# Forget gates of one attention layer: gate columns as the stationary operand on four column groups, tokens moving

## What is computed

```python
def fox_attention(h, w_in, f_bias, w_o):          # h: [1, 256, 1024], w_in: [1024, 3*1024 + 16]
    proj = h @ w_in
    q, k, v, f = jnp.split(proj, [D, 2 * D, 3 * D], axis=-1)      # f: [1, 256, 16], one gate a head
    log_f = jax.nn.log_sigmoid(f.astype(jnp.float32) + f_bias.astype(jnp.float32))
    F = jnp.cumsum(log_f, axis=1).transpose(0, 2, 1)
    ...
        logits = jnp.einsum('bhqd,bhkd->bhqk', qb, k).astype(jnp.float32) * scale
        logits = logits + Fq[..., :, None] - F[:, :, None, :]
    ...
```

## Time and profile before

| what | value |
|---|---|
| time, median of 3 runs | 2028.2 us (2025.67 to 2031.05) |
| profiled execution: span, first to last instruction | 2030.4 us |
| mean granted TensorE clock in it | 0.912 |
| instructions | 25040 |
| PE / PEld / DVE / ACT / POOL busy | 81% / 48% / 36% / 13% / 5% |
| HBM read | 578.88 MB, 286 GB/s over the span |

### The profile page before, as it was taken

How to read it: one execution, slowest core, us unless ns; L and a number is a source line. 1 busy time by engine, 2 the same in 40 slices (tenths; PEclk the granted TensorE clock), 3 DMA queues, 4 the chain that set the end, 5 groups by cost and what they waited for, 6 DMA issues and landing times.

```text
span 2030.4 us, 25040 instructions
## 1 busy us (share of the span) xinstructions
PE 1648.7 (81%) x10030; PEld 984.7 (48%) x10031; DVE 738.1 (36%) x1492; ACT 258.5 (13%) x630; POOL 94.1 (5%) x125
## 2 busy tenths in 40 slices
PE   5999987766665678876667547989999999999998
PEld 3754543222222254322222214766997486669963
DVE  2865452111101136211111003974467313444672
ACT  1002210000000021000000002232111122311100
POOL 1001001000000002910000000000000000000000
PEclk9989998888877799987887778999999999999999
DMA  9979479999999996999999987204435273204351
GB/s 362 402 314 413 172 305 412 421 422 422 422 422 422 405 389 272 415 405 422 421 422 422 422 332 291 84 1 176 166 125 207 104 259 144 105 11 166 125 209 40
DMA packets 122680, 581.33 MB, mean 286 GB/s; under 512 B 10820, under 2 KB 15272, under 8 KB 67160
## 3 DMA queue, kind: packets, MB, share of 16 engines
q1 hardware_dynamic: 120416, 573.92, 70.6%
q0 software_dynamic: 1104, 2.86, 0.4%
q10 hardware_dynamic: 1064, 3.17, 0.4%
HBM read 578.88 MB, written 1.05 MB: 286 GB/s over the span
## 4 chain that ended last, share of the span: by engine, by line
PE 35%; DMA 33%; PEld 14%; DVE 8%; issue 5%; ACT 2%; SPq 2%; PEldq 1%; DVEq 1%; ACTq 0%
DMA ring_buffer<-in_exp_w 29%; PEld ps L2175 10%; PE ps L1479 7%; PE ps L2204 6%; PE ps L1504 4%; PE ps L2893 4%; PE ps L2004 3%; DMA ring_buffer<-in_ada_w 2%; PEld ps L2146 2%; DMA ring_buffer<-in_attn_w_in 1%; PE ps L1004 1%; PE ps L2884 1%; SPq L1368 1%; PEld ps L831 1%; DVE xn L537 1%
## 5 line engine op out<-in xcount | busy, mean ns | idle before, releaser
L1479 PE MATMUL ps<-ring_buffer,arena 128*32 128x512 f32 x1984 | 295.8, 754 | 173.5 <-DMA ring_buffer<-in_exp_w 170.6
L1479 PEld LDWEIGHTS ps<-ring_buffer,arena 128*32 128x32 f32 x1984 | 76.8, 134 | 379.1 <-issue 324.7
L1504 PE MATMUL ps<-ring_buffer,arena 128*32 128x512 f32 x1088 | 151.8, 709 | 86.7 <-DMA ring_buffer<-in_exp_w 75.5
L1675 DVE TENSOR_TENSOR arena<-arena,ps 128x512 f32<-128x512 f32 x18 | 19.1, 1064 | 407.5 <-PE ps L1479 407.5
L2175 PE MATMUL ps<-arena,ring_buffer 128*128 128x128 f32 x1152 | 133.9, 276 | 3.7 <-issue 3.7
L2175 PEld LDWEIGHTS ps<-arena,ring_buffer 128*128 128x128 f32 x1152 | 130.8, 192 | 5.8 <-issue 5.8
L1504 PEld LDWEIGHTS ps<-ring_buffer,arena 128*32 128x32 f32 x1088 | 40.4, 127 | 186.8 <-issue 146.9
L2204 PE MATMUL ps<-ring_buffer,arena 128*128 128x512 f32 x252 | 111.0, 594 | 3.4 <-issue 1.9
L2175 PE MATMUL ps<-hT,ring_buffer 128*128 128x128 f32 x864 | 99.4, 275 | 0.0
L2175 PEld LDWEIGHTS ps<-hT,ring_buffer 128*128 128x128 f32 x864 | 97.9, 192 | 0.0
L1693 DVE TENSOR_TENSOR arena<-ps,gates 128x512 f32<-128x512 f32 x16 | 11.1, 692 | 193.7 <-PE ps L1504 193.7
(11 more groups left out here) (570 smaller groups left out, 2061.0 us busy)
## 6 DMA issues: line engine op xcount, KB each, us to landing
ring_buffer<-in_exp_w SPq DMA_DIRECT2D x376, 1024.0 KB, 18.6
ring_buffer<-in_ffn_w SPq DMA_DIRECT2D x30, 2048.0 KB, 11.8
ring_buffer<-in_ada_w SPq DMA_DIRECT2D x24, 2048.0 KB, 17.4
ring_buffer<-in_c_w_in SPq DMA_DIRECT2D x8, 2048.0 KB, 13.8
ring_buffer<-in_attn_w_in SPq DMA_DIRECT2D x6, 2048.0 KB, 16.0
arena<-in_exp_w SPq DMA_DIRECT2D x6, 1024.0 KB, 8.4
ring_buffer<-in_ab_w_in SPq DMA_DIRECT2D x3, 2048.0 KB, 14.1
ring_buffer<-in_ffn_w SPq DMA_DIRECT2D x6, 1024.0 KB, 6.3
```

What stands on the lines that cost most here:

```text
L1479: ins = pe.matmul(ps[c, bank, :], tokens[:, 4 * phase + k, c], halves[j][:, k, :], start=(phase == 0 and k == 0), stop=(phase == 1 and k = ...
L1504: ins = pe.matmul(ps[c, bank, :], tokens[:, 2 * phase + k, c], halves[j][:, k, half * 512:(half + 1) * 512], start=(phase == 0 and k == 0) ...
```

## The change

The gates are computed the other way round. The 16 gate columns of piece k are stationary and all 256 tokens move, and piece k goes to the column group 32 * (k % 4) of the array, so that the products of four pieces write to four different groups of PSUM partitions. Each group sums two pieces (k and k + 4). The four partial sums, with gates on partitions and tokens along the row, are copied by DVE to SBUF (`gate_parts`, in the buffer `probs`). Two products with `gate_parts` stationary (128 tokens each) and 16 columns of `fold` moving add the four groups and turn the result, so that tokens are on partitions as before. They go to bank 0, columns 64 to 95, and are placed in PE's order after the first two of the eight pieces of tile 17. DVE takes its bias addition from there. The counts of two semaphores move up by one. The wait for bank 0 moves from `gate_sums_pe` to the new `gate_fold_pe`.

```diff
+            gate_parts = probs[:, 0, 0, :]
+
+            def gate_fold_pe(pe):
                 bank_free(pe, SUM_BANK)
                 pe.wait_ge(gate_rows, 1)
+                for t in range(TT):
+                    ins = pe.matmul(ps[:, SUM_BANK, 64 + 16 * t:80 + 16 * t], gate_parts[:, t * P:(t + 1) * P],
+                                    const("fold")[:, 0:N_HEADS], start=True, stop=True)
+                ins.then_inc(gate_sums, 1)
+
+            def gate_sums_pe(pe):
+                pe.wait_ge(gate_rows, 2)
...
                 bank_free(pe, bank_of(F_TILE), F_TILE)
-                for t in range(TT):
-                    for k in range(KD):
-                        ins = pe.matmul(ps[:, bank_of(F_TILE), t * 16:(t + 1) * 16], hT[:, k, t * P:(t + 1) * P], w[:, k, :],
-                                        start=(k == 0), stop=(k == KD - 1))
+                for k in range(KD):
+                    g = 32 * (k % 4)
+                    ins = pe.matmul(ps[g:g + N_HEADS, bank_of(F_TILE), 0:S], w[:, k, :], hT[:, k, :],
+                                    start=(k < 4), stop=(k >= 4))
                 ins.then_inc(p_ready, 1)
                 release(pe)
                 w = ring.take(pe, ("attn_in", 4))
-                values_pe(pe, 17, w, 0, range(KD))
+                values_pe(pe, 17, w, 0, range(2))
+                gate_fold_pe(pe)
+                values_pe(pe, 17, w, 0, range(2, KD))
...
                 dve.wait_ge(p_ready, F_TILE + 1)
+                dve.tensor_copy(gate_parts, ps[:, bank_of(F_TILE), 0:S]).then_inc(gate_rows, 1)
                 dve.wait_ge(bias_loaded, 16)
-                v(dve.tensor_tensor(t1, ps[:, bank_of(F_TILE), 0:32].rearrange("p (t h) -> p t h", t=TT),
+                dve.wait_ge(gate_sums, 1)
+                v(dve.tensor_tensor(t1, ps[:, SUM_BANK, 64:96].rearrange("p (t h) -> p t h", t=TT),
                                     fbias.unsqueeze(1).to_broadcast([P, TT, N_HEADS]), ALU.add))
...
```

More of the change, by code:

```diff
@@ L798, in bank_free @@
                     pe.wait_ge(p_taken, before[-1] + 1)
-            def gate_sums_pe(pe):
+            gate_parts = probs[:, 0, 0, :]
+            def gate_fold_pe(pe):
                 bank_free(pe, SUM_BANK)
                 pe.wait_ge(gate_rows, 1)
+                for t in range(TT):
[4 more added lines that the diff above has]
+                pe.wait_ge(gate_rows, 2)
                 pe.matmul(ps[:, SUM_BANK, 0:16], const("upto"), lf[:, 0, :], start=True, stop=True)
@@ L807, in gate_turn_pe @@
             def gate_turn_pe(pe):
-                pe.wait_ge(gate_rows, 2)
+                pe.wait_ge(gate_rows, 3)
                 for t in range(TT):
@@ L907, in proj_dve @@
                 values(18)
-                dve.wait_ge(gate_sums, 1)
+                dve.wait_ge(gate_sums, 2)
                 dve.tensor_copy(F, ps[:, SUM_BANK, 0:32].rearrange("p (t h) -> p t h", t=TT)).then_inc(gate_rows, 1)
@@ L911, in proj_dve @@
                 condition_unit(9)
-                dve.wait_ge(gate_sums, 2)
+                dve.wait_ge(gate_sums, 3)
                 for row in (0, 32):
```

## The result

The changed kernel takes 2011.06 us (median of 8 runs, 2007.97 to 2014.6), the kernel before 2021.98 us (8 runs, 2013.17 to 2031.05). The ratio is 0.9948, with a 95% interval of 0.9925 to 0.9972. A second measurement, with more runs of both, gave 0.9951 (0.9929 to 0.9973). So the change makes the kernel faster by 0.5%, some 10 us, where 5.4 were forecast (2022.8 against 2028.2, a ratio of 0.9973). The median of the kernel before had itself come down from 2028.2 (three runs) to 2022.0 (eight) and later 2020.2 (35): the forecast of the saving and the base it was taken from were both off.

A forecast was written before the change was run, and what follows sets the result against it. No single limit: PE and transfers each hold a third of the wait chain, PE's pace sets the projection stage's end. 3.46 (products) - 0.5 (fold) + 2.45 (clock) = 5.4 us; 2028.2 - 5.4 = 2022.8 us, range 2018.6 to 2028.1.

The forecast's parts named there:

- Products: Gate products on PE: eight on four column groups take 1.32 us where the old took 4.78, saving 3.46 us.
- Fold and its cover: Two fold products on PE add 0.5 us; 0.9 us of cover from tile 17 hides the wait for DVE's copy.
- Rival 5: The fold waits for a late DVE copy, PE idles 4.3 us and the clock falls; 2029.6 us, chance 0.03.
- Clock: Tiles 17 and 18 behind the gates run at full clock, saving 2.45 us (bounds 0 and 2.45).
- The rival that the fall isn't in every execution: The clock falls anyway, or other executions didn't lose by it; gain 3.0 us, 2025.2 us, chance 0.24.
- the stated bounds of 4.5 to 5.6: Range put around the forecast saving of 5.4 us, which was given a chance of 0.50.
- What is late next: Behind the gates' stage: the full 5.4 us passes through conditioning transfers, heads and expert loads to the kernel's end.
- Rival 3: The saving is given back later by expert loads that start when they did; 2028.2 us, chance 0.08.
- rival 2: The column groups don't overlap: gates take 3.8 us, gain 2.9 us; 2025.3 us, chance 0.04.
- Rival 4: More than forecast: clock falls at 136.3 and the heads' start move to where they cost nothing; 2021.1 us, chance 0.11.
- The size: Whole kernel: 5.4 us less than the 2028.2 us median of three runs, so 2022.8 us.

The follow-up runs named there:

- fold_first: Changed kernel with the fold right behind the gate products, ahead of all of tile 17, so nothing covers DVE's copy; ratio 0.9962, median 2013.29 us.
- before: The kernel before, without the change; median 2021.98 us of 8 runs.
- before_plus2: Kernel before with two small products, result unused, added behind PE's first transposes to move its later code; ratio 0.9985.
- before_plus10: Kernel before with ten small products, result unused, added behind PE's first transposes to move its later code; ratio 0.9978.
- pad58: Kernel before with 58 small products, result unused, added behind PE's first transposes to move its later code; ratio 1.0032.
- bunch: Changed kernel with the sixteen old narrow gate products put back as dead work ahead of the new ones; 2023.73 us, one run.
- after_again: Changed kernel measured and traced once more, no edit; ratio 0.9951, median 2011.32 us of 12 runs.
- before_third: Kernel before traced a third time, no edit, one run; the execution of 2022.93 us.
- after: The changed kernel in its first measurement and trace; ratio 0.9948, median 2011.06 us of 8 runs.
- pad6: Changed kernel with six small products, result unused, behind PE's first transposes, giving PE as many products as the kernel before; ratio 0.9973.
- after_plus5: Changed kernel with five small products, result unused, added behind PE's first transposes; ratio 0.9968.
- before_again: Kernel before measured and traced a second time, no edit; ratio 1.0002, median 2019.71 us of 12 runs.
- one_group: Changed kernel with all eight gate products on the first column group and the fold taking that group alone; ratio 0.9966, median 2014.25 us.
- spread: Kernel before with the old narrow gate products placed one behind each wide product of key tiles 14 and 15; ratio 0.9987, median 2017.94 us.

## Why the prediction was right and wrong

**Products: right.** Forecast 1.32 us from the gates' start to the values', from L550's row; measured 1.33. The bound of no overlap (3.8 us) was near what one group takes (3.61 and the 0.26 behind).

**Fold and its cover: right.** Forecast 0.5 us without a wait; measured 0.36 to 0.52 and no wait. But "were the cover gone, every us of lateness would be one on PE" was wrong: fold_first's wait of 1.13 us cost 2.6, since the clock fell too. Rival 5 had that mechanism, and fold_first shows it on a small scale.

**Clock: right in mechanism, and its upper end in size.** No fall within tiles 17 and 18 in the changed kernel, in four of four traces with the gates on four groups and the fold covered. The rival that the fall isn't in every execution is settled: all six traces with the old bunch ahead of the values (three of before, before_plus2, before_plus10, pad58) have it, with a stage of 41.2 to 41.3 us in three and 39.76 in three. So the stage's saving is 5.5 or 4.0 us, by where the fall lands, and 4.8 in the mean, where 5.4 was taken; the stated bounds of 4.5 to 5.6 follow from no sum of the terms' own bounds (0.3 to 5.5). Of the Trainium skill's rule that idle gaps cost the clock ("TensorE: Matmul & The Clock Gate", "Why this matters for your kernels"): fold_first, with 1.13 us of idle ahead of a fall, points its way, though that gap is shorter than those that the page speaks of; before and bunch, where PE was never idle for more than 0.35 us ahead of the fall, show that it isn't the whole rule.

**What is late next: half right.** L573 was forecast at 124.4 and came at 123.35, from key tiles that began 0.83 earlier; the last conditioning unit landed at 175.25 (forecast 176). The first expert transfer row was forecast at 292.6 and stands at 295.06, since a fall of the clock in the output projection took 1.7 us of that execution (15.54 against 13.84) and a lower clock from 256 to 264 us another 1.1 (L265 4.63 for 3.83 us, L1456 3.83 for 3.58). Such falls differ between executions of the same code: the same group takes 13.84 us in after_again, and 15.54 in before_third. The saving did pass through the transfer-bound stages: by the start of one same matmul near 1100 us, the four traces with the changed gates and the cover (after, after_again, pad6, after_plus5) lie at 1095.8, 1093.5, 1096.7 and 1099.0, five of the old gates (three of before, before_plus2, before_plus10) at 1099.3, 1099.1, 1102.1, 1101.1 and 1103.7. The means are 1096.3 and 1101.0, 4.8 apart. Rival 3 is out, and so is rival 2 by L850's row. Rival 4's sign was right, but not its mechanism: the falls it named are still there at times.

**The size: wrong, for a step that wasn't there.** The step that failed is 2028.2 - 5.4: it puts the difference of everything behind the gates' stage at nothing, without having read its rows, and it hangs on a base of three runs. What the runs show in its place is 4 to 6 us more, of which the gates' stage has none. Part of them is in the second experts' stage: in part of its executions the kernel before spends 9 us in one branch. Of its 35 runs beside the first experiments 23 lie at 2012.8 to 2021.0 with a median of 2017.5, and 12 at 2025.6 to 2033.4. The lower group against after_again: 2017.5 - 2011.3 = 6.2 us, close to the forecast. The whole against it: 2020.2 - 2011.3 = 8.9 us. So not quite 3 of the 8.9 us go to the upper group that the changed kernel doesn't have. Of the other 6.2 the stage has 4.8; the stages behind 1300 us differ by 1 to 2 us in the mean of the traces, but their ranges overlap (711 to 716 us with the old gates, 711 to 714 with the new). That the upper group is the long branch fits its size and the traces (executions of 2030.46 and 2027.94 us have it, one of 2022.93 doesn't), but I have no trace of each run, so it is inferred. Nor are the groups always apart: the 29 runs of before beside the second experiments have the same gap (none from 2021.4 to 2026.3, 11 above it), the 29 beside the third have runs at 2021.9, 2022.4, 2022.5, 2024.3, 2024.8 and 2025.0.

The row was there to be read: 16.77 us of issue where the first experts' stage has 8.50 for the same lines. I had looked only at stages that the change reaches, and a change of code length moves all later code. The second fault is the base: three runs at 2025.7 to 2031.0 were taken for the kernel's spread, and by their size they were of the upper group; the range, hung on their median, missed a kernel whose runs reach from 2013 to 2034. A smaller fault is the profiled execution's 2.2 us above the median: that set a span beside times, and in the other runs the time is 1.8 to 2.0 us above the span.

**Open.** What the 4 to 6 us beyond the stage are: the long branch, by the medians, accounts for not quite 3 of them, and only if the upper group is that branch. Why an execution has the long branch and another of the same kernel has not, and whether the changed kernel is free of it for good or by its present length: with five small products added its runs spread to 2021.3 and with six to 2026.6, so its 2007 to 2015 isn't a property of the gates alone. Whether the clock would fall behind fewer narrow products than these sixteen wasn't tried. No version tried beats the changed kernel.

## What to carry to other kernels

Small products in a bunch cost twice: their own weight loads, and the clock of what follows; make the wide operand the moving one and spread what must stay narrow, and cover a small wait with wide products, since 1.13 us of idle beside narrow work cost 2.6. Compare like stages of the kernel before, layer by layer, before taking all that is not edited as constant: an unexplained idle piece may be gone, or come, with a change that has nothing to do with it. To price an edit alone, keep the length of the code, as pad6 does. Take the base and its spread from many runs: here three lay in the upper part of a spread of 20 us.

## What the runs showed of the hardware

- Four column groups ran eight products of 16 by 256 in 1.06 us, one group in 3.61: 3.4 times.
- The granted clock fell to 0.50 with PE never idle for more than 0.35 us, when the work was 128-column loads with 16 columns moving for 2.4 to 3.7 us (before, before_again, and bunch, where 1.06 us of the new gate products came between). It stayed at 1.00 when 16 columns were stationary and 256 moved for 3.6 us (one_group), and when each narrow product stood behind a wide one (spread).
- Products on four column groups between full-array ones cost no time that shows: 0.26 or 0.35 us of idle ahead of L850 and 0.28 behind it, where a release alone has 0.25 to 0.35.
- A branch of PE in a loop took 5.9 to 6.4 us where its like took 0.2, in thirteen of the fourteen traces in the second experts' stage. In three of them a second one took 9.2 to 9.5 us, and there five instruction fetches of 16 KB stand from 1170 to 1205 us, where before_third and after have three.
